# Router of a mixture-of-experts layer: x2 turned in contiguous runs, the last tile's first half turned early, its row scaling behind the expert choice

## Chip, cores and metric

One core of one Trainium2 chip runs the whole kernel. The time is device microseconds of one launch. The engines are TensorE (PE in the rows, PEld for its weight loads), VectorE (DVE), ScalarE (ACT), GpSimd (POOL) and SyncE (SP); the last two also issue the DMAs, each on a queue of its own.

## What is computed

A two-part encoder layer on 512 prompt rows and 256 sample rows of 1024 channels, 768 rows in all: six tiles of 128 rows. The first part (projection, differential attention, retention, merge, output projection) ends in the residual sum x2. The second part is a mixture of 32 experts, and the change sits at the seam between the two:

```
x = x + token_mixer(rmsnorm(x, attn_norm_g), ...)          # this sum is x2
xt = rmsnorm(x, ffn_norm_g)
lg = xt @ w_rg + b_rg                                      # 4 groups: the best one
le = einsum('td,gde->tge', xt, w_re) + b_re                # 8 experts in it: the best two
h = silu(xb @ w1[e]) * (xb @ w3[e]);  y = (h @ w2[e]) * gate
out = x + sum of a token's two experts;  then a last rmsnorm
```

## The kernel before

The program is written engine by engine, and each engine runs its list in the order written. Semaphores join the lists: s_w counts finished halves of the output projection, s_x2 halves of x2, s_rTm and s_rTc halves of x2 turned and copied, s_lg logits, s_rx logits scaled on VectorE, s_rr scaled rows, s_nb the finished routing tables.

**The output projection and the router's logits** run tile by tile, t from 0 to 5. TensorE sums each half n of a tile (512 columns, 24 matmuls: each operand is split into a high and a low part, L584 to L586) in PSUM bank 6 or 7. VectorE adds the residual row by row (L1561), which is x2. TensorE turns x2 with eight 128x128 transposes (`route_columns`, L772 to L780), four into bank 0 and four into bank 1; the slice of each has a stride of 8 elements, `x2[t % 3][:, 4 * j + c::KC]`. ScalarE copies each bank into `rT` (`route_copy`, L1108 to L1114). Eight small matmuls give the 36 logits of each row in bank 2 (`logits`, L782 to L791), and VectorE scales them by the row's 1/rms and adds the bias (`route_logits`, L1502). `logits` waits on s_rx, since bank 2 has to be read before it is written again. In the loop, `route_columns(t-1)` stands behind the first half of tile t and `logits(t-1)` in the middle of its second half; the last tile's turns and logits come behind the loop. The router's weights are laid out on the host, and multiplied on GpSimd by the norm's gains (`gcol`, L1724).

**The scaled rows.** ScalarE squares a tile's x2 (L1127), VectorE works out 1/rms (`rsqrt_column`, nine small operations from L1242) and writes the scaled rows `rrow` (L1568), and GpSimd stores them twice in DRAM (`xn_scratch`, L1728). In the list of VectorE the row scaling of tile t stands ahead of the logits of tile t-1; for the last tile both logits follow it:

```
dve.scalar_tensor_tensor(out=rrow[t % 2][:, :], in0=x2[t % 3][:, :], ...).then_inc(s_rr, 1)
if t >= 1:
    route_logits(t - 1)
...
route_logits(NT - 1)
choose(NT - 2, NT)
```

**The choice.** `choose` (L1509 to L1548) picks each row's experts: for tiles 0 to 3 ahead of the last tile's sum, for tiles 4 and 5 at the end. TensorE counts rows per expert (`count`, L829 and L833), VectorE works out slots and one-hot tables (L1582 to L1604), TensorE turns them into the index table (L844), and VectorE writes it (`idxt`, L1622). Three idle matmuls (`keep_busy`, L825) run ahead of the wait for it.

**The first block of the expert stage.** GpSimd gathers 64 pairs of half rows by `idxt` (L1748), TensorE turns them (L859), VectorE copies them (`xT`, L1639), and TensorE starts on w1 and w3 (L869). The weights come through `rawe`, a ring of three experts, 2 MB per matrix, issued by SP (L520). SP issues expert 1 (6 MB) once the last half of the projection is summed (s_w), behind it the store of the last tile's x2 (`x2_out`, L536, 0.5 MB), then, after s_rr, w1 of expert 2, and the rest after the first gather. ScalarE copies the first expert's weights out of the ring: half of w1 and w3 (`first_up(0)`, L1131), then w2 (L1143), then two exponentials for the gates, then the other half. The first of these copies waits for all stores of x2, because it writes over x2's buffer; the second waits for the stores of the scaled rows. VectorE computes the gates (L1625 to L1629) ahead of the `xT` copy of the first block. The stage then runs 41 blocks, of which each needs w1, w3 and w2 of its expert.

Of the kernel before, what the change touches and what calls it, by code (L numbers as in the profile page):

```python
# [19 lines left out]
ALU = mybir.AluOpType  # L20
# [3 lines left out]
P = 128  # L24
D = 1024
KC = D // P
SEQS = (512, 256)
T = sum(SEQS)
NT = T // P
# [6 lines left out]
NG, EPG = 4, 8  # L36
NE = NG * EPG
# [63 lines left out]
def hybrid_layer(nc, A):  # L101
# [19 lines left out]
    x2 = [at(f"x2{s}", D_O + (32 + 4 * s) * KB, [P, D]) for s in range(3)]  # L121
# [15 lines left out]
    rstd = small("rstd", [P, 48])  # L137
# [59 lines left out]
    g2 = at("g2", D_O + 16 * KB, [P, D])  # L197
    rT = at("rT", D_O + 44 * KB, [P, KC, P])
    rrow = [at(f"rrow{s}", F_O + (16 + 4 * s) * KB, [P, D]) for s in range(2)]
    wrt = at("wrt", F_O + 36 * KB, [P, KC, NG + NE])  # L200
    brt = at("brt", F_O + 36 * KB + 1280, [P, NG + NE])
    gcol = at("gcol", F_O + 36 * KB + 1152, [P, KC])
# [36 lines left out]
    ps = [ctx.enter_context(nc.psum_tensor(f"ps{i}", [P, 512], F32)) for i in range(8)]  # L239
# [4 lines left out]
    ident = C("ident")  # L244
# [11 lines left out]
    with ctx:  # L256
# [58 lines left out]
        s_x2 = sem("s_x2")  # L315
        s_x2s = [sem(f"s_x2s{s}") for s in range(3)]
        s_x2l = sem("s_x2l")
        s_rp = sem("s_rp")
# [3 lines left out]
        s_rr = sem("s_rr")  # L322
        s_rst = [sem(f"s_rst{s}") for s in range(2)]
        s_rTm = sem("s_rTm")
# [92 lines left out]
        def _(sp):  # L417
# [89 lines left out]
            for k in range(2, 2 * NT):  # L507
                gate_half(k)
                if k in (3, 4, 11):
                    p = {3: 5, 4: 6, 11: 7}[k]  # L510
# [3 lines left out]
            sp.dma_start(g2[:, :], A["ffn_norm_g"].partition_broadcast(P)[:, 0, :]).then_inc(s_rp, 16)  # L514
            sp.dma_start(wrt[:, :, :], A["router_w"].rearrange("(p c) n -> p c n", c=KC)).then_inc(s_rp, 16)
            sp.dma_start(brt[:, :], A["router_b"].rearrange("(a n) -> a n", a=1).partition_broadcast(P)[:, 0, :]).then_inc(s_rp, 16)
            sp.dma_start(gcol[:, :], A["ffn_norm_g"][0].rearrange("(p c) -> p c", c=KC)).then_inc(s_rp, 16)
            def weight(x, slot, k, done):
                c = slot * EW + k * 2 * PIECE
                sp.dma_start(rawe[:, c:c + 2 * PIECE].rearrange("p (h n) -> p h n", h=2),  # L520
# [60 lines left out]
        def _(pe):  # L581
# [187 lines left out]
                        mm = pe.transpose(ps[4 + n % 2][:, c * P:(c + 1) * P], mg[t][:, 4 * j + c::KC], ident)  # L769
                    mm.then_inc(s_mT, 1)  # L770

            def route_columns(t):  # L772

                pe.wait_ge(s_x2, 2 * t + 2)
                if t >= 1:
                    pe.wait_ge(s_rTc, 2 * t)
                for j in range(2):
                    for c in range(4):
                        mm = pe.transpose(ps[j][:, c * P:(c + 1) * P], x2[t % 3][:, 4 * j + c::KC], ident)
                    mm.then_inc(s_rTm, 1)  # L780

            def logits(t):  # L782
                pe.wait_ge(s_rTc, 2 * t + 2)
                if t == 0:
                    pe.wait_ge(s_wrg, 1)
                if t >= 1:
                    pe.wait_ge(s_rx, t)
                for c in range(KC):
                    mm = pe.matmul(ps[2][:, 0:NG + NE], rT[:, c, :], wrt[:, c, :],
                                   start=(c == 0), stop=(c == KC - 1))  # L790
                mm.then_inc(s_lg, 1)  # L791
            merged_to_columns(0)
            for t in range(NT):
                if t + 1 < NT:
                    merged_to_columns(t + 1)
                pe.wait_ge(s_mTl, 2 * t + 2)
                for n in range(2):
                    if t >= 1:
                        pe.wait_ge(s_x2, 2 * t + n - 1)
                    for j in range(2):  # L800
                        p = 2 * n + j
                        if t == 0:
                            pe.wait_ge(s_lo, ZP + 4 + p + 1)
                        for k in range(4):
                            c = 4 * j + k
                            mm = split_mm(ps[6 + n][:, :], mTh[t % 2][:, c, :], mTl[t % 2][:, c, :],
                                          m_hi[4 + p][:, k * 512:(k + 1) * 512],
                                          m_lo[4 + p][:, k * 512:(k + 1) * 512],
                                          c == 0, c == KC - 1)
                        if t == NT - 1 and j == 0:  # L810
                            mm.then_inc(s_pe, 1)
                        if t >= 1 and n == 1 and j == 0:
                            logits(t - 1)
                    mm.then_inc(s_w, 1)
                    if t >= 1 and n == 0:
                        route_columns(t - 1)
            route_columns(NT - 1)


            picked = Ab[:, :, :].rearrange("p t e -> p (t e)")  # L820
# [92 lines left out]
        def _(act):  # L913
# [191 lines left out]
                    act.activation(mTh[t % 2][:, 4 * j:4 * j + 4, :].rearrange("p c k -> p (c k)"),  # L1105
                                   ps[4 + n % 2][:, :], ACT.Copy).then_inc(s_mTh, 1)

            def route_copy(t):  # L1108
                for j in range(2):
                    act.wait_ge(s_rTm, 2 * t + j + 1)  # L1110
                    if t >= 1:
                        act.wait_ge(s_lg, t)
                    act.activation(rT[:, 4 * j:4 * j + 4, :].rearrange("p c k -> p (c k)"),
                                   ps[j][:, :], ACT.Copy).then_inc(s_rTc, 1)  # L1114
# [3 lines left out]
            for t in range(NT):  # L1118
                if t + 1 < NT:
                    merged_hi(t + 1)  # L1120
                if t >= 1:
                    route_copy(t - 1)

                act.wait_ge(s_x2, 2 * t + 2)
                if t >= 2:
                    act.wait_ge(s_rst[t % 2], 16 * (t // 2))
                act.activation(rrow[t % 2][:, :], x2[t % 3][:, :], ACT.Square, accum_out=ssq[:, t:t + 1]).then_inc(s_sq2, 1)  # L1127
            route_copy(NT - 1)

            def first_up(h):  # L1130
                act.activation(cur13[h][:, :, :], rawe[:, 0:4 * PIECE].rearrange("p (k n) -> p k n", k=2)  # L1131
# [80 lines left out]
        def _(dve):  # L1212
# [289 lines left out]
            def route_logits(t):  # L1502
                dve.wait_ge(s_lg, t + 1)
                dve.scalar_tensor_tensor(out=lg[:, t, :], in0=ps[2][:, 0:NG + NE], scalar=rstd[:, t:t + 1],
                                         in1=brt[:, :], op0=ALU.mult, op1=ALU.add).then_inc(s_rx, 1)
# [3 lines left out]
            def choose(a, b):  # L1509
# [36 lines left out]
                                              op0=ALU.mult, op1=ALU.add))  # L1546
                pick(A12[:, 1, a:b, :], v[:, 6, :])
                dve.tensor_tensor(Ab[:, a:b, :], A12[:, 0, a:b, :], A12[:, 1, a:b, :], ALU.add).then_inc(s_Ab, 1)  # L1548
            BIG = 1.0e30
            for t in range(NT):  # L1550
                if t + 1 < NT:
                    merged_lo(t + 1)
                else:
                    choose(0, NT - 2)
                dve.wait_ge(s_xr[t % 3], 16 * (t // 3 + 1))
                for n in range(2):
                    dve.wait_ge(s_w, 2 * t + n + 1)
                    if t >= 3 and n == 0:
                        dve.wait_ge(s_rTm, 2 * (t - 2))
                        dve.wait_ge(s_x2s[t % 3], 16)  # L1560
                    dve.tensor_tensor(x2[t % 3][:, n * 512:(n + 1) * 512], ps[6 + n][:, :],  # L1561
                                      xres[t % 3][:, n * 512:(n + 1) * 512], ALU.add).then_inc(s_x2, 1)

                dve.wait_ge(s_sq2, t + 1)
                rsqrt_column(t, D)
                if t == 0:
                    dve.wait_ge(s_rp, 16 * 4)
                dve.scalar_tensor_tensor(out=rrow[t % 2][:, :], in0=x2[t % 3][:, :], scalar=rstd[:, t:t + 1],  # L1568
                                         in1=g2[:, :], op0=ALU.mult, op1=ALU.mult).then_inc(s_rr, 1)
                if t >= 1:  # L1570
                    route_logits(t - 1)

            route_logits(NT - 1)
            choose(NT - 2, NT)
            dve.memset(zero[:, :], 0.0).then_inc(s_ini, 1)
            dve.wait_ge(s_ini, 1)
            link(dve.tensor_tensor(v6[:, 2, :], v6[:, 6, :], v6[:, 5, :], ALU.subtract))
# [234 lines left out]
```

## Time and profile before

| | us |
|---|---|
| median of 3 runs | 1207.0 (1206.47 to 1207.01) |
| the profiled execution, its own time | 1205.33 |
| its span, first to last instruction | 1203.5 |
| TensorE busy | 1093.9 (91%) |
| VectorE busy | 520.1 (43%) |
| ScalarE busy | 400.6 (33%) |
| GpSimd busy | 189.1 (16%) |

The profiled execution is one run; what it took beyond its span is 1.8 us. Busy shares are means over all stages. A row of the timeline has the start in us, the time in us, the engine, the line, the operation, output <- input, the shape and the count; in brackets stands the idle time just before it and what ended it. A row of the chain has the start, the time and what the end of the program was waiting for in that stretch.

### The profile page before, as it was taken

How to read it: one execution, taken by the hardware profiler on the slowest of the kernel's cores; microseconds unless marked ns; L12 is line 12 of the kernel's file. 1: busy time of each engine (PE TensorE's matmuls, PEld its weight loads, DVE VectorE, ACT ScalarE, POOL GpSimd, SP SyncE). 2: the span in 40 equal slices, each digit the busy share in tenths (PEclk: the TensorE clock that was granted, in tenths of full speed). 3: DMA queues.
4: the chain of work that ended last, by engine and by line, in shares of the span. 5: the costliest groups of instructions: out<-in, count | busy, mean ns of one | idle time of the engine just before them, and what ended most of it. 6: DMA issues, size and time to landing. Idle time of an engine off the chain costs nothing.

```text
span 1203.5 us, 15505 instructions
## 1 busy us (share of the span) xinstructions
PE 1093.9 (91%) x5142; PEld 660.6 (55%) x5142; DVE 520.1 (43%) x893; ACT 400.6 (33%) x629; POOL 189.1 (16%) x236
## 2 busy tenths in 40 slices
PE   5899999999999998999977999999998798999960
PEld 4688888888876667878863333333333233333320
DVE  5651522111027898563354435352443343341518
ACT  5322233222135666112214243424143323333232
POOL 0110011011000000000001232333233323232210
PEclk9999999999999999999987999999999999999995
DMA  8733331621341005448358899999999999999546
GB/s 312 256 123 123 114 122 48 240 104 44 139 170 58 1 2 175 158 152 360 123 219 357 351 422 419 419 420 420 420 413 420 421 421 419 419 422 419 225 158 260
DMA packets 69248, 308.89 MB, mean 257 GB/s; under 512 B 9024, under 2 KB 9152, under 8 KB 43872
## 3 DMA queue, kind: packets, MB, share of 16 engines
q1 hardware_dynamic: 56144, 273.86, 57.2%
q0 software_dynamic: 13072, 34.63, 7.4%
q8 instruction: 17, 0.28, 0.1%
q14 instruction: 15, 0.12, 0.0%
HBM read 278.57 MB, written 39.06 MB: 264 GB/s over the span
## 4 chain that ended last, share of the span: by engine, by line
PE 69%; DMA 14%; DVE 9%; ACT 4%; issue 3%; SPq 1%; DVEq 0%; ACTq 0%; POOLq 0%; POOL 0%
PE ps L869 18%; PE ps L584 12%; PE ps L586 12%; PE ps L585 12%; DMA rawe<-in_w 10%; PE ps L896 8%; DMA x_scratch<-x 2%; PE ps L859 2%; DVE cur13b L1662 1%; PE ps L878 1%; ACT prob L1013 1%; DMA xrow<-in_x_sample 1%; DVE att L1366 1%; ACT cur L1194 1%; DMA ya<-y_scratch 1%
## 5 line engine op out<-in xcount | busy, mean ns | idle before, releaser
L584 PE MATMUL ps<-whi,xTh 128*128 128x512 f32 x480 | 188.4, 393 | 18.1 <-DVE wlo L1225 13.8
L585 PE MATMUL ps<-wlo,xTh 128*128 128x512 f32 x480 | 187.9, 392 | 0.0
L586 PE MATMUL ps<-whi,xTl 128*128 128x512 f32 x480 | 187.9, 391 | 0.0
L869 PE MATMUL ps<-cur13a,xT 128*64 128x512 f32 x656 | 157.5, 624 | 2.0 <-DVE xT L1639 1.7
L1662 DVE COPY cur13a<-rawe 128x4096 f32 x31 | 71.2, 2296 | 191.3 <-DMA rawe<-in_w 99.7
L869 PE MATMUL ps<-cur13b,xT 128*64 128x512 f32 x656 | 147.8, 592 | 0.0
L896 PE MATMUL ps<-cur,hT 128*64 128x512 f32 x640 | 146.2, 598 | 0.0
L1194 ACT ACTIVATE cur<-rawe 128x4096 f32 x31 | 112.1, 3618 | 3.7 <-issue 1.4
L584 PEld LDWEIGHTS ps<-whi,xTh 128*128 128x128 f32 x480 | 91.0, 190 | 37.3 <-issue 18.5
L963 ACT ACTIVATE zst<-ps,rstd 128x512 f32<-128x512 f32 x60 | 41.1, 687 | 208.0 <-PE ps L586 205.9
L585 PEld LDWEIGHTS ps<-wlo,xTh 128*128 128x128 f32 x480 | 91.0, 189 | 19.1
L586 PEld LDWEIGHTS ps<-whi,xTl 128*128 128x128 f32 x480 | 90.8, 189 | 19.0
L869 PEld LDWEIGHTS ps<-cur13b,xT 128*64 128x64 f32 x656 | 47.8, 137 | 93.0 <-issue 93.0
L869 PEld LDWEIGHTS ps<-cur13a,xT 128*64 128x64 f32 x656 | 46.1, 143 | 83.0 <-issue 77.0
L1225 DVE TENSOR_TENSOR wlo<-raw,whi 128x2048 fp32r<-128x2048 f32 x20 | 45.8, 2292 | 104.2 <-ACT whi L919 103.3
L1744 POOL COPY idxb<-idxt 128x1 int32 (+1 forms) x40 | 45.4, 1135 | 241.9 <-PE ps L859 241.9
L896 PEld LDWEIGHTS ps<-cur,hT 128*64 128x64 f32 x640 | 42.4, 136 | 73.4 <-issue 68.5
L1721 POOL DMA_DIRECT2D z_scratch<-zst x60 | 32.9, 548 | 316.5 <-ACT zst L963 171.6
L1662 DVE COPY cur13b<-rawe 128x4096 f32 x31 | 71.1, 2292 | 23.3 <-PE ps L869 23.2
L1176 ACT ACTIVATE ystage<-ps 128x512 f32<-128x512 f32 x41 | 24.5, 597 | 159.3 <-PE ps L896 159.3
L1639 DVE COPY xT<-ps 128x512 f32<-128x512 f32 x41 | 28.1, 684 | 84.8 <-PE ps L859 84.8
L1164 ACT ACTIVATE sg<-ps 128x256 f32<-128x256 f32 x41 | 15.7, 383 | 141.4 <-PE ps L869 141.4
(212 smaller groups left out, 1382.6 us busy)
## 6 DMA issues: line engine op xcount, KB each, us to landing
rawe<-in_w SPq DMA_DIRECT2D x96, 2048.0 KB, 25.9
raw<-in_w_in SPq DMA_DIRECT2D x20, 1024.0 KB, 6.2
z_scratch<-zst POOLq DMA_DIRECT2D x60, 256.0 KB, 2.3
gat<-z_scratch SPq DMA_DIRECT2D x12, 512.0 KB, 3.8
xn_scratch<-rrow POOLq DMA_DIRECT2D x6, 1024.0 KB, 5.2
ya<-y_scratch SPq DMA_DIRECT2D x6, 1024.0 KB, 10.7
raw<-in_w_out SPq DMA_DIRECT2D x4, 1024.0 KB, 6.6
xcol<-in_x_cols SPq DMA_DIRECT2D x6, 512.0 KB, 10.2
```

What stands on the lines that cost most here:

```text
L584: pe.matmul(out, ah, bh, start=first, stop=False)
L585: pe.matmul(out, ah, bl, start=False, stop=False)
L586: return pe.matmul(out, al, bh, start=False, stop=last)
L869: mm = pe.matmul(ps[0][u * CAP:(u + 1) * CAP, :], xT[:, c, h * CAP:(h + 1) * CAP], cur13[h][:, :, c * 512 + u * 256:c * 512 + u * 256 + 25 ...
L896: mm = pe.matmul(ps[6][u * CAP:(u + 1) * CAP, :], hT[:, k, h * CAP:(h + 1) * CAP], w2, start=(h == 0 and k == 0), stop=(h == 1 and k == 1))
L963: act.activation(zst[k][:, :], ps[k][:, :], ACT.Sigmoid if c >= 6 else ACT.Copy, scale=rstd[:, t:t + 1]).then_inc(s_zev, 1)
L1194: act.activation(cur2[:, :], rawe[:, bass.ds((e % RING) * EW + 4 * PIECE, 2 * PIECE)], ACT.Copy).then_inc(s_cw2, 1)
L1225: dve.tensor_tensor(elo[slot][:, :], raw[slot_raw][:, :], hi[:, :].bitcast(F32), ALU.subtract).then_inc(s_lo, 1)
L1639: dve.tensor_copy(xT[:, :, :].rearrange("p c k -> p (c k)"), ps[2][:, :]).then_inc(s_xt, 1)
L1662: dve.tensor_copy(cur13[h][:, :, :], pair[:, :, h * PIECE:(h + 1) * PIECE]).then_inc(s_c13, 1)
L1721: pool.dma_start(z_d[t * P:(t + 1) * P, c * 512:(c + 1) * 512], zst[k][:, :]).then_inc(s_zst[k], 16)
L1744: pool.tensor_copy(idxb[:, :], idxt[:, bass.ds(b, 1)]).then_inc(s_ic, 1)
```

## The change

The transposes of x2 read runs of 128 columns in place of every eighth column; the router's weights and gains are laid out on the host to match. `route_columns` takes a half. For the last tile its first half is turned in the middle of the last half's sum, behind `logits(4)`, and ScalarE copies it before it squares that tile's rows. On VectorE `route_logits(4)` moves up between the two residual sums of the last tile, and the row scaling of the last tile moves behind the second `choose`.

```diff
-            sp.dma_start(gcol[:, :], A["ffn_norm_g"][0].rearrange("(p c) -> p c", c=KC)).then_inc(s_rp, 16)
+            sp.dma_start(gcol[:, :], A["ffn_cols"].rearrange("(p c) -> p c", c=KC)).then_inc(s_rp, 16)
...
-            def route_columns(t):
-
-                pe.wait_ge(s_x2, 2 * t + 2)
+            def route_columns(t, j):
+
+                pe.wait_ge(s_x2, 2 * t + j + 1)
                 if t >= 1:
                     pe.wait_ge(s_rTc, 2 * t)
-                for j in range(2):
-                    for c in range(4):
-                        mm = pe.transpose(ps[j][:, c * P:(c + 1) * P], x2[t % 3][:, 4 * j + c::KC], ident)
-                    mm.then_inc(s_rTm, 1)
+                for c in range(4):
+                    mm = pe.transpose(ps[j][:, c * P:(c + 1) * P], x2[t % 3][:, (4 * j + c) * P:(4 * j + c + 1) * P], ident)
+                mm.then_inc(s_rTm, 1)
...
                         if t >= 1 and n == 1 and j == 0:
                             logits(t - 1)
+                            if t == NT - 1:
+                                route_columns(t, 0)
                     mm.then_inc(s_w, 1)
                     if t >= 1 and n == 0:
-                        route_columns(t - 1)
-            route_columns(NT - 1)
+                        route_columns(t - 1, 0)
+                        route_columns(t - 1, 1)
+            route_columns(NT - 1, 1)
...
-            def route_copy(t):
-                for j in range(2):
+            def route_copy(t, halves=(0, 1)):
+                for j in halves:
...
                 if t >= 1:
                     route_copy(t - 1)
+                if t == NT - 1:
+                    route_copy(t, (0,))
...
-            route_copy(NT - 1)
+            route_copy(NT - 1, (1,))
...
+            def rows_scaled(t):
+                dve.scalar_tensor_tensor(out=rrow[t % 2][:, :], in0=x2[t % 3][:, :], scalar=rstd[:, t:t + 1],
+                                         in1=g2[:, :], op0=ALU.mult, op1=ALU.mult).then_inc(s_rr, 1)
...
                                       xres[t % 3][:, n * 512:(n + 1) * 512], ALU.add).then_inc(s_x2, 1)
+                    if t == NT - 1 and n == 0:
+                        route_logits(t - 1)
...
-                dve.scalar_tensor_tensor(out=rrow[t % 2][:, :], in0=x2[t % 3][:, :], scalar=rstd[:, t:t + 1],
-                                         in1=g2[:, :], op0=ALU.mult, op1=ALU.mult).then_inc(s_rr, 1)
-                if t >= 1:
-                    route_logits(t - 1)
+                if t < NT - 1:
+                    rows_scaled(t)
+                    if t >= 1:
+                        route_logits(t - 1)
 
             route_logits(NT - 1)
             choose(NT - 2, NT)
+            rows_scaled(NT - 1)
...
-        [inputs["w_rg"][0][:, None, order], inputs["w_re"][0][order].transpose(1, 2, 0)], axis=1).reshape(D, NG + NE))
+        [inputs["w_rg"][0][:, None, order], inputs["w_re"][0][order].transpose(1, 2, 0)], axis=1).reshape(KC, P, NG + NE).transpose(1, 0, 2).reshape(D, NG + NE))
+    laid["ffn_cols"] = _np.ascontiguousarray(inputs["ffn_norm_g"][0].reshape(KC, P).T.reshape(D))
```

TensorE before, in the middle of the last half of tile 5 (`wrt,rT` are the logits of tile 4, `mhi`, `mlo` the projection's weights, `x_75` is x2 of tile 5):

```order
L789 MATMUL ps<-wrt,rT 128x36 [waits s_rx,s_rTc]
L789 MATMUL ps<-wrt,rT 128x36 x7
L584 MATMUL ps<-mhi_155,mTh_70 128x512
L585 MATMUL ps<-mlo_160,mTh_70 128x512
L586 MATMUL ps<-mhi_155,mTl_72 128x512
```

The same place in the changed kernel:

```order
L788 MATMUL ps<-wrt,rT 128x36 [waits s_rx,s_rTc]
L788 MATMUL ps<-wrt,rT 128x36 x7
L778 MATMUL ps<-cst,x_75 128x128 [waits s_rTc,s_x2]
L778 MATMUL ps<-cst,x_75 128x128 x3
L584 MATMUL ps<-mhi_155,mTh_70 128x512
L585 MATMUL ps<-mlo_160,mTh_70 128x512
L586 MATMUL ps<-mhi_155,mTl_72 128x512
```

Four of the eight transposes of tile 5 now stand, with a wait for the first half of x2, ahead of the last 12 matmuls of the projection.

VectorE before, from the first choice's end over the last tile's two residual sums (the nine small operations of 1/rms follow them):

```order
L1548 TENSOR_TENSOR Ab<-A_175 128x128 [waits s_dv]
L1561 TENSOR_TENSOR x_75<-ps,xres_165 128x512 [waits s_rTm,s_x2s2,s_w,s_xr2]
L1561 TENSOR_TENSOR x_75<-ps,xres_165 128x512 [waits s_w]
L1242 TENSOR_SCALAR rs_a<-ssq 128x1 [waits s_sq2]
L1243 TENSOR_SCALAR ssq<-ssq 128x1
```

and behind 1/rms:

```order
L1247 SCALAR_TENSOR_TENSOR rstd<-rs_a,rstd 128x1 [waits s_dv]
L1568 SCALAR_TENSOR_TENSOR rrow_169<-x_75,rstd,g_166 128x1024 [waits s_dv]
L1504 SCALAR_TENSOR_TENSOR lg<-ps,rstd,brt 128x36 [waits s_lg] x2
L1522 TENSOR_REDUCE v_93<-lg 128x2 [waits s_rx]
L1523 TENSOR_TENSOR gq<-lg,v_93 128x8 [waits s_dv]
```

VectorE in the changed kernel, from the same first row:

```order
L1552 TENSOR_TENSOR Ab<-A_175 128x128 [waits s_dv]
L1568 TENSOR_TENSOR x_75<-ps,xres_165 128x512 [waits s_rTm,s_x2s2,s_w,s_xr2]
L1508 SCALAR_TENSOR_TENSOR lg<-ps,rstd,brt 128x36 [waits s_lg]
L1568 TENSOR_TENSOR x_75<-ps,xres_165 128x512 [waits s_w]
L1246 TENSOR_SCALAR rs_a<-ssq 128x1 [waits s_sq2]
```

and from the second choice's end:

```order
L1552 TENSOR_TENSOR Ab<-A_175 128x64 [waits s_dv]
L1554 SCALAR_TENSOR_TENSOR rrow_169<-x_75,rstd,g_166 128x1024
L1585 MEMSET zero 128x32
L1587 TENSOR_TENSOR v_93<-v_93 128x6 [waits s_ini]
L1592 TENSOR_SCALAR wint<-ps 128x32 [waits s_dv,s_rk]
```

The logits of tile 4 are scaled before the second sum, and the row scaling (L1554 in the changed kernel) stands between the choice and the slot arithmetic.

## Rows read from the trace of the kernel before

**Rows 1.** The chain that ended last, from the projection's end to the second weight copy.

```profile
617.77 0.38 SPq L520
...
619.22 20.09 DMA x_scratch<-x
...
639.42 0.06 ACT cur13a L1131
...
642.94 0.14 ACT cur L1143
```

**Rows 2.** The timeline of TensorE, 612 to 650 us.

```profile
613.02 1.87 PE L789 MATMUL ps<-wrt,rT 128*128 128x36 f32 x16
...
618.52 1.16 PE L779 MATMUL ps<-cst,x 128*128 128x128 f32 x8 [0.78 <-DVE x L1561]
...
623.06 1.95 PE L789 MATMUL ps<-wrt,rT 128*128 128x36 f32 x16 [1.90 <-DVE lg L1504]
...
647.15 0.75 PE L859 MATMUL ps<-cst,xg 128*128 128x128 f32 x4 [0.36 <-DMA xg<-xn_scratch,idxt]
649.65 3.65 PE L869 MATMUL ps<-cur13a,xT 128*64 128x512 f32 x16 [1.75 <-DVE xT L1639]
```

**Rows 3.** The timeline of VectorE, 614 to 643 us.

```profile
614.65 0.68 DVE L1561 TENSOR_TENSOR x<-ps,xres 128x512 f32<-128x512 f32 x1
...
621.46 1.28 DVE L1568 SCALAR_TENSOR_TENSOR rrow<-x,rstd,g 128x1024 f32<-128x1024 f32 x1
...
625.05 0.26 DVE L1504 SCALAR_TENSOR_TENSOR lg<-ps,rstd,brt 128x36 f32<-128x36 f32 x1 [2.13 <-PE ps L789]
...
631.42 0.19 DVE L1582 TENSOR_SCALAR wint<-ps 128x32 uint32<-128x32 f32 x1 [1.34 <-PE ps L833]
...
642.45 0.28 DVE L1622 TENSOR_SCALAR idxt<-ps,cst 128x56 int32<-128x56 f32 x1 [1.26 <-PE ps L844]
```

**Rows 4.** The timelines of ScalarE and GpSimd, 618 to 645 us.

```profile
619.55 1.06 ACT L1113 ACTIVATE rT<-ps 128x512 f32<-128x512 f32 x2
...
623.04 0.68 POOL L1728 DMA_DIRECT2D xn_scratch<-rrow  x1 [12.95 <-DVE rrow L1568]
...
643.68 1.10 POOL L1748 DMA_INDIRECT xg<-xn_scratch,idxt  x1 [7.13 <-DVE idxt L1622]
```

**Rows 5.** Landing of L1728's stores, then queues (packets, MB, share) in 626 to 635 us.

```profile
DMA to landing us min/median/max: 4.4/5.2/12.9
...
q1 hardware_dynamic: 335, 2.61, 73.2%
q0 software_dynamic: 265, 1.04, 28.1%
```

**Rows 6.** Stretches: busy PE, PEld, DVE, ACT, POOL, then PEclk, DMA share, GB/s.

```profile
625.00:646.00 21.00, 11.65 (x38) 8.52 (x38) 13.91 (x66) 6.58 (x2) 1.62 (x2) 0.51 0.91 368
660.00:662.00 2.00, 2.00 (x6) 0.47 (x4) 0.00 (x0) 0.00 (x1) 0.00 (x0) 0.50 1.01 426
690.00:1132.00 442.00, 420.57 (x1908) 149.31 (x1906) 173.75 (x161) 149.73 (x168) 130.49 (x141) 0.98 1.00 414
```

**Rows 7.** The chain in the first blocks of the expert stage.

```profile
659.49 8.70 PE ps L869 x32
...
672.89 7.02 PE ps L869 x32
```

**Rows 8.** SP's own waits, 600 to 700 us.

```profile
SPq L520 <- ACT cur L1194: 17.3, 1, 17.3
```

**Rows 9.** Turns of x2 (L779) and of z (L627): the chain's steps, then weight loads in ns.

```profile
609.55 0.88 PE ps L779 x8
...
348.30 7.87 PE ps L627 x72
...
L779 PEld LDWEIGHTS ps<-cst,x x48: 185/188/208, 551.8 to 619.3; 128*128 128x128 f32 x48
...
L627 PEld LDWEIGHTS ps<-cst,zqk x48: 138/141/143, 347.9 to 354.9; 128*128 128x128 f32 x48
```

## The prediction

> **What bounds the kernel now.** I began at the end and asked what has to be earlier for the program to end earlier. In the windows from 690 to 1132 us the DMA share is 1.00, at 414 GB/s [rows 6]: the expert stage is a weight stream with full queues. Such a stream ends earlier only if it starts earlier. SP's own waits tell what starts it: after the first experts SP stood 17.3 us until ScalarE had copied w2 out of the ring [rows 8], a copy that stands behind the first blocks' matmuls. So a shift of the first block (the `xT` copy, then L869 at 649.65) reaches the end one for one, and nothing ahead of it counts unless it moves that start.
>
> Two branches lead to the first block, and the change speaks to one of them.
>
> Branch A, the routing: residual sum, turns, logits, choice, counts, tables. TensorE's logits of tile 5 start at 623.06 after an idle 1.90 us that VectorE's scaling of the logits of tile 4 ended [rows 2]; VectorE scales those of tile 5 at 625.05, has waited 1.34 us for the counts at 631.42, and writes `idxt` from 642.45 to 642.73 [rows 3]. GpSimd issues the gather at 643.68 [rows 4], TensorE turns the rows from 647.15 to 647.90 and then waits 1.75 us [rows 2].
>
> Branch B, the weights of the first expert: the chain of work that ended last goes this way [rows 1]. The last matmul of the projection lets SP issue expert 1 at 617.77, three transfers of 2 MB; the store of the last x2 is issued behind them at 619.22 and takes 20.09 us. ScalarE then copies from 639.42 and from 642.94, computes the exponentials, VectorE the gates, and only then comes `xT`. From landing (639.31) to the first L869 (649.65) are 10.3 us, all in series. Branch A had its columns ready at 647.90, and the first L869 follows such a point by an `xT` copy of 0.7 us: A has about 1.0 us of slack. B ends last.
>
> **The change, part by part.**
>
> The order of the columns. The projection's stage is bound by TensorE, so 40 transposes of tiles 0 to 4 lie on its path. Eight strided ones step in 0.88 us, 110 ns each; 72 contiguous ones of the earlier stage in 7.87 us, 109 ns each [rows 9]. Worth 0. The strided loads do take longer (188 against 141 ns) but run beside the matmul ahead.
> [...]
>
> The transposes inside the last sum. Tile 4's logits end at 613.02 + 1.87 = 614.89 [rows 2] and the last 12 matmuls followed at once. The first half of x2 is done only at 614.65 + 0.68 = 615.33, since VectorE runs the first choice ahead of it [rows 3]. TensorE now waits 0.44 us, then 0.06 to start and 4 x 0.11 to turn, with some 0.1 for the start of a group (eight after a wait took 1.16 for 0.88): the last sum ends **1.1 us later** (0.9 to 1.3), 618.9. This is on branch B: s_w lets SP issue expert 1, and everything of B is behind it.
>
> The routing. x2's second half is 1.1 later (619.6). ScalarE squares (1.2 us) and copies one half, not two (1.06 us for two [rows 4]): `rT` is complete at about 621.3. The logits of tile 4 are scaled already at 615.6, between the two sums, where VectorE idles. So TensorE's logits of tile 5 start at 621.4 and not 623.06, and the scaling that was at 625.05 comes at 623.4: 1.6 us earlier. The moved row scaling (1.28 us [rows 3]) lies in the 1.34 us for which VectorE waits for the counts; without this cover it would cost 1.3. `idxt` is done at about 641.1, **1.6 us earlier**. This is branch A, which had slack: worth nothing by itself.
>
> The scaled rows. They end at 629.6 instead of 622.74, so GpSimd's store of 1 MB is issued at 629.8, not 623.04 [rows 4], and SP's w1 of expert 2, behind s_rr, as much later; the queue is full of expert 1 until about 637, so that load loses no time. The store took 12.9 us where its kind takes 5.2 [rows 5]. As long it would land at 642.7, when w1 alone is left beside it; I take 641. ScalarE's second copy, which waits for it, can't start before 643.7; the gather, which waits for it too, needs it by about 641. Hidden, or nearly.
>
> The last x2's store. In 626 to 635 us the scaled rows' queue moved 1.04 MB and SP's 2.61 MB [rows 5]: the 1 MB store goes through ahead of x2's. In the changed kernel it starts about 6.7 us later, at 633, and has moved about 7 us x 1.04/9 = 0.8 MB when x2's store lands. What is not yet moved, 0.2 MB at some 0.4 MB/us, gives back 0.5 us, and less if the two stores alternate more evenly. Landing is later by 1.1 - 0.5 to 1.1: I take **+0.8 us**, 640.1.
>
> The sum. Branch B: 640.1 + 10.3 = 650.4 for the first L869. Branch A: gather at 642.1, columns 4.2 us later (as from 643.68 to 647.90) at 646.3, or 647.3 beside the stream. B still ends last, and the program is later by 0.8 us. The profiled execution's 1205.33 becomes 1206.1; it lay 1.7 below the median of the runs, and the median 1207.0 becomes **1207.8 us**. About 0.2% (2.4 us) is what a measurement of this kernel can tell from no change, so this is no change that shows.
>
> **The rivals.**
>
> A colder first block (slower). TensorE's granted clock stood at 0.51 of full through 625 to 646, and again at 0.50 in 660 to 662 [rows 6]: the latter after a block with TensorE idle for part of it, and it made the 32 matmuls of block 2 8.70 us instead of 7.02 [rows 7], 1.7 us. With A earlier and B later, TensorE idles 4 us ahead of the first L869 where it idled 1.75. [...] For it: this longer idle time. Against it: the clock held at full from 646 on with 1.75 us of idling.
>
> Late rows (slower, and plainly so). The store of the scaled rows now starts late; if it lands more than 14 us after its issue (643.8), first ScalarE's w2 copy, soon the gather wait for it, and each us beyond costs one. At 17 us it is 3 us on top of nothing else: 1210.8. For it: 12.9 us last time. Against it: by then expert 1 is through, and less stands beside it.
>
> The store of x2 gets ahead (faster). If the scaled rows' packets start later than I assume, x2's store passes before nearly all of them: 1.05 MB less at 0.4 MB/us is 2.5 us less, +1.1 - 2.5 = -1.4, and A allows it, being 1.6 earlier: 1205.5. The same time comes out if, against the chain, the routing ended last. It speaks for it that x2's transfer stands in the queue before the rows are even issued; against it that at 633 some 3 us of expert 1 are still ahead.
>
> Strides cost (faster). If the steps hide a price that the loads show, 47 ns for each of 44 transposes on TensorE's path are 2.1 us, and the time is 1205.7. Rows 9 speak against it.
>
> **How the numbers follow.** Forecast 0.60, a colder first block 0.14, late rows 0.06, x2's store ahead 0.15, strides 0.05. The forecast's own bounds are +0.3 to +1.4, with the scatter of the runs (0.5) 1206.8 to 1208.8. The range reaches to the colder block above and to the two faster cases below: 1205.0 to 1209.8. Slower by over 0.2% (above 1209.4) are half of the colder blocks and most late rows, 0.13; faster (below 1204.6) is a faster case with a clock that doesn't fall in block 2, 0.05; the rest, 0.82, is within.
>
> **What would show it.** Right: the four turns inside the last sum behind 0.4 us of waiting, SP's expert 1 at 618.9, logits of tile 5 on VectorE at 623.4, `idxt` at 641.1, x2's store landing at about 640, L869 at 650.4 with TensorE idle for 4 us ahead of it, and the chain through the store of x2. Wrong: a chain through `xn_scratch` or the gather; L869 before 649; a window at clock 0.50 after 650; a number of blocks other than 41, since the new order of the sums could turn a near tie in the router.

## The result, and the profile after

| | before | changed |
|---|---|---|
| median of 20 runs, us | 1206.85 (1203.79 to 1208.97) | 1210.19 (1206.92 to 1212.60) |
| ratio, with its 95% interval | | 1.0028 [1.0019, 1.0037] |
| the profiled execution, us | 1205.33 | 1208.01 |
| its span, us | 1203.5 | 1206.2 |

The kernel became slower by 0.28%, outside the range, and the likeliest case of the prediction (+0.8 us, nothing to be seen) did not happen. The profiled execution shows how. All times below stand against one anchor that every version has: the start of TensorE's logits of tile 4, 613.02 us in the kernel before [rows 2] and 613.31 in the changed one. Ahead of it the programs do the same work. "The first block" is, on TensorE, its 32 matmuls of w1 and w3.

TensorE's timeline of the changed kernel, from that anchor to the first block:

```profile
613.31 1.87 PE L788 MATMUL ps<-wrt,rT 128*128 128x36 f32 x16
...
615.69 0.66 PE L778 MATMUL ps<-cst,x 128*128 128x128 f32 x4 [0.51 <-DVE x L1568]
...
619.89 0.66 PE L778 MATMUL ps<-cst,x 128*128 128x128 f32 x4 [0.79 <-DVE x L1568]
...
621.87 1.95 PE L788 MATMUL ps<-wrt,rT 128*128 128x36 f32 x16
...
647.07 0.75 PE L861 MATMUL ps<-cst,xg 128*128 128x128 f32 x4 [0.77 <-DMA xg<-xn_scratch,idxt]
651.54 5.97 PE L871 MATMUL ps<-cur13a,xT 128*64 128x512 f32 x16 [3.73 <-DVE xT L1649]
```

Second and third row: four turns stand inside the last sum behind a wait of 0.51 us, four behind it. Fourth row: the logits of tile 5 start 8.6 us behind the anchor, 10.0 before. Then the two differences that matter: the first block waits 3.73 us for `xT` where it waited 1.75 [rows 2], and its first 16 matmuls take 5.97 us where they took 3.65.

The chain that ended last, of the changed kernel:

```profile
620.59 20.62 DMA x_scratch<-x
...
651.54 9.41 PE ps L871 x32
...
663.71 7.02 PE ps L871 x32
```

It goes through the store of the last x2 as before [rows 1], and the transit (issue to landing) is 20.62 us, not 20.09. The 32 matmuls of the first block take 9.41 us. In the chain of the kernel before they took 7.09:

```profile
649.65 7.09 PE ps L869 x32
```

Those of the second block take 7.02 us and not 8.70 [rows 7]. The windows show why (columns as in [rows 6]):

```profile
646.00:649.40 3.40, 1.04 (x5) 0.56 (x4) 0.62 (x4) 3.40 (x4) 0.79 (x1) 1.00 0.53 135
649.40:652.80 3.40, 1.26 (x4) 0.53 (x6) 0.95 (x3) 3.23 (x2) 0.24 (x1) 0.51 0.97 407
652.80:656.20 3.40, 3.40 (x10) 0.95 (x8) 0.00 (x0) 1.02 (x2) 0.00 (x0) 0.50 1.02 421
656.20:659.40 3.20, 3.20 (x16) 0.98 (x14) 0.00 (x0) 0.00 (x0) 0.00 (x0) 0.99 1.02 433
```

The second of these windows in the kernel before:

```profile
649.40:652.80 3.40, 3.15 (x16) 1.16 (x18) 0.19 (x1) 2.36 (x3) 0.31 (x1) 1.00 0.95 398
```

The granted clock is back at full at 646 in both kernels (1.00 over 646.00 to 649.40). In the changed one TensorE then idles, and at 649.4 the clock falls to 0.50 of full and stays there until 656.

The routing did what it should, and the scaled rows are late as planned:

```profile
641.24 0.28 DVE L1632 TENSOR_SCALAR idxt<-ps,cst 128x56 int32<-128x56 f32 x1 [1.25 <-PE ps L846]
```

```profile
630.23 0.68 POOL L1738 DMA_DIRECT2D xn_scratch<-rrow  x1 [19.85 <-DVE rrow L1554]
641.98 0.52 POOL L1744 MEMSET xg<- 128x512 f32 x1 [11.07 <-DMA xn_scratch<-rrow]
643.49 1.10 POOL L1758 DMA_INDIRECT xg<-xn_scratch,idxt  x1 [0.98 <-POOL xg L1744]
```

The first row is of VectorE's timeline, the others are of GpSimd's. VectorE scales the rows at 628.66, and GpSimd issues their store at 630.23. `idxt` starts 27.93 us behind the anchor, 29.43 before [rows 3]: 1.5 us earlier. The gather starts only 0.5 us earlier against the anchor (30.2 for 30.7 [rows 4]): GpSimd cleared its tile only once the scaled rows had landed.

### The profile page after: what moved, and what is told of

Same layout as the page of the kernel before. It is cut to its first block, busy times and chain, and to the rows that moved or that the text cites. A ratio compares the mean times of both kernels' runs of the same rounds, so it can differ in the third digit from the quotient of the medians.

```text
span 1206.2 us, 15511 instructions
## 1 busy us (share of the span) xinstructions
PE 1097.5 (91%) x5142; PEld 661.8 (55%) x5142; DVE 520.1 (43%) x893; ACT 400.7 (33%) x629; POOL 192.4 (16%) x236
## 4 chain that ended last, share of the span: by engine, by line
PE 67%; DMA 15%; DVE 10%; issue 4%; ACT 3%; SPq 1%; DVEq 0%; ACTq 0%; POOLq 0%; POOL 0%
PE ps L871 18%; PE ps L584 12%; PE ps L586 12%; PE ps L585 12%; DMA rawe<-in_w 11%; PE ps L898 7%; DMA x_scratch<-x 2%; PE ps L861 1%; DVE cur13b L1672 1%; PE ps L880 1%; ACT prob L1015 1%; DMA xrow<-in_x_sample 1%; DVE att L1370 1%; DMA ya<-y_scratch 1%; DVE mx L1357 1%
## 5 line engine op out<-in xcount | busy, mean ns | idle before, releaser
L871 PE MATMUL ps<-cur13a,xT 128*64 128x512 f32 x656 | 160.8, 635 | 4.0 <-DVE xT L1649 3.7
L1168 ACT ACTIVATE sg<-ps 128x256 f32<-128x256 f32 x41 | 15.7, 384 | 144.8 <-PE ps L871 144.8
## 6 DMA issues: line engine op xcount, KB each, us to landing
ya<-y_scratch SPq DMA_DIRECT2D x6, 1024.0 KB, 10.6
```

Source lines behind the costliest of these rows:

```text
L871: mm = pe.matmul(ps[0][u * CAP:(u + 1) * CAP, :], xT[:, c, h * CAP:(h + 1) * CAP], cur13[h][:, :, c * 512 + u * 256:c * 512 + u * 256 + 25 ...
```

## The experiments

The same five readings stand for every run: start of the first block's matmuls behind the anchor, idle time of TensorE just ahead of them, time of the first and the second block's 32 matmuls (from the chain, or, where the chain leaves the block out, from the timeline), and the rest of the span behind the anchor (the profiled span less the anchor). A block is called cold where its matmuls ran in part at the lower clock (0.50 of full in the windows), warm where they took 7.0 to 7.1 us. The part ahead of the anchor took 612.8 to 617.2 us in the profiled executions, though it is the same work in all: in some the granted clock was still at 0.50 in 45 to 48 and in 366 to 369 us (`logits_only`), in others at 1.00 (`after_warm`). It adds scatter to every median and says nothing of the change; so a profile is compared by the last column, and the medians decide. The last column is one execution each, and scatters too: `best_busy` and `best_busy_again` are one program, with 586.3 and 588.5.

| run | first block at | idle ahead | block 1, block 2 | rest of span | ratio to before, interval |
|---|---|---|---|---|---|
| before | 36.63 | 1.75 | 7.09, 8.70 | 590.5 | |
| changed | 38.23 | 3.73 | 9.41, 7.02 | 592.9 | 1.0028 [1.0019, 1.0037] |
| columns_only | 36.65 | 1.72 | 8.62, 7.02 | 590.5 | 1.0000 [0.9991, 1.0010] |
| turn_only | 37.66 | 0.94 | full speed, 7.02 | 589.9 | 1.0015 [1.0002, 1.0027] |
| logits_only | 36.67 | 3.85 | 10.00, 8.71 | 592.9 | 1.0029 [1.0017, 1.0042] |
| rows_only | 36.36 | 2.10 | 10.06, 8.71 | 593.1 | 1.0016 [1.0004, 1.0029] |
| after_warm | 38.11 | 1.12 | 7.09, 7.02 | 590.3 | 1.0009 [0.9995, 1.0023] |
| logits_warm | 36.66 | 1.35 | 7.09, 7.02 | 589.4 | 1.0002 [0.9993, 1.0011] |
| store_first_before | 35.53 | 0.78 | full speed, 7.02 | 589.6 | 1.0009 [1.0000, 1.0018] |
| logits_store_first | 34.32 | 0.78 | full speed, 7.02 | 588.7 | 0.9991 [0.9980, 1.0002] |
| no_early_turn | 37.01 | 3.79 | 9.63, 7.02 | 592.3 | 1.0036 [1.0023, 1.0048] |
| rows_ahead | 37.80 | 3.98 | 9.12, 7.02 | 592.2 | 1.0043 [1.0030, 1.0056] |
| best_busy | 34.03 | 0.78 | full speed, 7.02 | 586.3 | 0.9989 [0.9977, 1.0001] |
| best_stream | 37.69 | 0.78 | 9.19, 7.02 | 592.1 | 1.0034 [1.0021, 1.0047] |
| no_early_warm | 37.20 | 1.42 | 7.09, 7.02 | 589.4 | 0.9988 [0.9978, 0.9998] |
| no_busy | 36.61 | 1.48 | 8.70, 7.02 | 590.5 | 1.0013 [0.9997, 1.0029] |
| best_busy_again | 34.33 | 0.78 | full speed, 7.02 | 588.5 | 0.9986 [0.9974, 0.9998] |

**The four parts, one at a time.** Theory at this point: the turns inside the last sum delay SP's transfers. Rivals: the late store of the scaled rows, and the clock.

`columns_only`, the new column order alone, with both halves of the last tile turned behind the sum (the diff is against the changed kernel):

```diff
-                            if t == NT - 1:
-                                route_columns(t, 0)
...
+            route_columns(NT - 1, 0)
             route_columns(NT - 1, 1)
```

The matching edit on ScalarE and the two edits on VectorE are undone as well.

> Only the order of the columns changes, with the laid out weights; both halves of the last tile are turned behind the sum and both other edits are undone. If the steps of the transposes are what counts (110 ns for eight, as for contiguous ones): the same time as before, the first L869 at 649.5 to 650, and weight loads of the turns at 141 instead of 188 ns that buy nothing. If strides cost TensorE time: 2 us faster. If the new layout itself is what made the changed kernel slower: 3 us slower.

1207.24 us, ratio 1.0000. The column order costs and gives nothing. In its profile the clock fell to 0.50 at about 649.9 and was back at 1.00 from 653.6, and the first block took 8.62 us, behind 1.72 us of idling; in the kernel before the clock held through 1.75.

`turn_only`, the same with the first half turned inside the last sum:

> Contiguous columns and the first half of the last tile turned inside the last sum; the logits of tile 4 and the row scaling stay where they were before. First theory (the wait and the four turns inside the sum delay SP's expert 1 and the store of x2 behind it): the last sum ends 1.1 us later than in the kernel before, the store lands 1.1 later, the first L869 starts 1.1 later, the time is 1 to 1.5 us longer. Rival (the late store of the scaled rows does the harm): within 0.3 us of before in the landing after correcting for the sum, and the loss of the changed kernel mostly absent.

1208.80 us, +0.15% [0.02, 0.27]. The first block starts 37.66 us behind the anchor, 1.03 later than in the kernel before, with a transit of 20.1: the first theory's 1.1 us is there. The routing is late too, since tile 5's logits start 1.1 us later and take 2.87 us for 1.95; the two branches end within 0.2 us of each other, and the chain names the routing. The scaled rows were stored ahead of the choice here, so a late store of them is not the cause. That the 1.1 us alone make the 0.15% is not shown: in the profile block 2 ran warm and the rest of the span is 0.6 us shorter than before, and the runs fall in two groups, 5 at 1205.6 to 1207.2 with a mean granted clock of 0.964 to 0.966, and 7 at 1208.1 to 1211.6 with 0.959 to 0.964, as would come of a clock that falls in some runs.

`logits_only`, the kernel before with tile 4's logits scaled between the sums:

```diff
                                       xres[t % 3][:, n * 512:(n + 1) * 512], ALU.add).then_inc(s_x2, 1)
+                    if t == NT - 1 and n == 0:
+                        route_logits(t - 1)
...
-                if t >= 1:
+                if 1 <= t < NT - 1:
                     route_logits(t - 1)
```

> The kernel before with one edit: the logits of tile 4 are scaled between the two residual sums of the last tile. First theory: the routing tables end 2.2 us earlier (about 640.5) and nothing follows, since the store of x2 lands at 639.3 as before and the first L869 stays at 649.7: time the same. Rival (the clock): TensorE idles 2 us longer ahead of the first block, its clock falls there more often, and the median is 0.5 to 1.7 us longer with the same start of the first block.

1211.12 us: +0.29% [0.17, 0.42], the whole loss of the changed kernel from an edit that only removes waiting. Its chain and a window of it:

```profile
622.98 20.14 DMA x_scratch<-x
...
653.45 10.00 PE ps L869 x32
```

```profile
653.00:659.00 6.00, 5.55 (x14) 1.71 (x16) 0.40 (x1) 2.57 (x3) 0.00 (x0) 0.50 1.02 425
```

The transit of the store and the start of the first block (36.67) are those of before. All that moved on the way to it is the routing, and with it TensorE's idle time, 3.85 us for 1.75; the first block takes 10.00 us, with the clock at 0.50 in 653 to 659. The rival with the clock is what happened, at more than its upper price.

`rows_only`, the kernel before with the last row scaling behind the choice (its old place is dropped):

```diff
             choose(NT - 2, NT)
+            rows_scaled(NT - 1)
```

> The kernel before with one edit: the row scaling of the last tile stands behind the second choice. The tables end 1.3 us earlier, the store of the scaled rows is issued about 6.5 us later. First theory by the bytes ahead of it: the store of x2 lands 0 to 0.5 us earlier and the time is the same or 0.5 us less. Rival (the two stores clash, as a transit of 20.6 in place of 20.1 us in the changed kernel suggests): x2's store lands 0.5 us later or more and the time is 0.5 to 1 us longer.

1208.72 us, +0.16% [0.04, 0.29]. The transit was 19.83 us and the first block 0.3 earlier, so the two stores did not clash. But the time is 1.5 us longer, which neither theory had: the first block is cold again (10.06). TensorE idled only 2.10 us just ahead of it. The clock fell to 0.50 with this and with 1.72 us in `columns_only`, and held at 1.00 with 1.75 in the kernel before, so the length of the last idle stretch does not decide by itself whether it falls.

**The clock held up.** `after_warm` and `logits_warm` put three idle matmuls into the gap:

```diff
             rows_to_columns(0)
+            keep_busy(3)
             up(0)
```

> The changed kernel with three idle matmuls (the same as the three behind the index tables, on bank 7) between the turns of the first gathered rows and the first block: they fill the 3.7 us for which TensorE idles there. Theory of the clock: the first block runs at full clock, 7.1 instead of 9.4 us, though it starts no earlier (38.2 us behind the logits of tile 4), and the median falls by 1.5 to 2.5 us to about 1208, 0.5 to 1.5 above the kernel before, which is what the turns in the last sum and the longer transit cost. Rival (the transfers: the late store of the scaled rows holds up the store of x2, and this is the whole loss): no gain, 1210.

> The kernel before with the logits of tile 4 scaled early, and the same three idle matmuls ahead of the first block. Theory of the clock: the 0.3% that the early scaling alone had lost is gone, the first L869 starts 36.7 us behind the logits of tile 4 and takes 7.1 us for 32; time within 0.1% of before, or a little under where the second block keeps the clock too. Rival (the early tables hurt in another way, as by a gather that collides with the weight stream): still 3 to 4 us above before.

```profile
646.46 0.75 PE L861 MATMUL ps<-cst,xg 128*128 128x128 f32 x4 [0.72 <-DMA xg<-xn_scratch,idxt]
647.04 2.74 PE L827 MATMUL ps<-cst 128*128 128x512 f32 x6
650.90 3.65 PE L871 MATMUL ps<-cur13a,xT 128*64 128x512 f32 x16 [1.12 <-DVE xT L1650]
```

These are TensorE's rows of `after_warm`: the fillers take 2.74 us, the block starts as late as in the changed kernel (38.11) and runs at 3.65 us per 16 matmuls. The median was 1206.81, against 1206.70 of the kernel before measured beside it: +0.09% [-0.05, 0.23], 1.1 us, within the forecast's 0.5 to 1.5. For `logits_warm` it was +0.02% [-0.07, 0.11], and 0.29% without the fillers. Nothing but idle matmuls was added, the first block started within about 0.1 us of where it did without them, and both blocks ran at full clock (granted 1.00, 7.09 and 7.02 us), so the loss was the clock. The kernel before with the same fillers was not run; as its own second block was cold (8.70), part of what the fillers gave here they might give there too.

**What is left without it.** `no_early_turn` is the changed kernel without the turns in the last sum, `rows_ahead` the changed kernel with the row scaling back ahead of the logits of tile 5.

> The changed kernel with both halves of the last tile turned behind the sum, as before; early logits of tile 4 and late row scaling stay. If the turns inside the sum cost 1.1 us on the branch of the store and the cold first block costs the rest: the first L869 starts 36.4 to 37.2 us behind the logits of tile 4 (38.2 in the changed kernel), the first block is still cold (about 10 us), and the time is 1 us under the changed kernel's, near 1209. Rival (the turns are harmless, the clock is all): 1210 as the changed kernel.

> The changed kernel with the last tile's row scaling back ahead of the logits of tile 5. The scaled rows are stored 5 us earlier, ahead of the last x2. If the late store of the rows lengthened the transit of x2's store by 0.5 us: transit 20.1, first L869 at 37.7 behind the logits of tile 4, the clock still low in the first block, and 0.5 us under the changed kernel, 1209.5. Rival (the transit is chance): 20.5 as in the changed kernel and the same 1210.

Both starts came as expected or near it (37.01, and 37.80 with a transit of 20.2), both first blocks were cold, and both medians (1210.52 of 6 runs and 1211.34 of 5) are above the changed kernel's, where 1209 and 1209.5 were expected: two misses. A cold first block cost 1.5 to 3.0 us over all profiles, depending on when the clock falls and rises (1.5 where it was at 0.50 from 649.9 to 653.3, `columns_only`; 3.0 where it was from 651.8 to 658.6, `rows_only`), and that can hide a difference of 0.5 or 1 us. Inconclusive by themselves; hence the pair with a warm block:

> The changed kernel without the turns inside the last sum and with three idle matmuls ahead of the first block. If both causes are real (clock, and the turns' 1.1 us): the first L869 starts 37.0 us behind the logits of tile 4 against 38.1 with the turns, takes 7.1 us, and the median is 0.5 to 1 us under that of the same kernel with the turns, at the level of before (ratio 1.000). Rival (only the clock matters): the same as with the turns, 1.0009.

1206.06 us, ratio 0.9988 [0.9978, 0.9998]. The same kernel with the turns (`after_warm`) has 1.0009 [0.9995, 1.0023]: the turns cost 0.2% between them, somewhat more than their 0.9 us of start; the intervals overlap a little, so this is likely and not clear of noise. Without the turns and with the fillers the changed kernel is faster than the one before, which had no such fillers.

`no_busy` takes the kernel before and drops its own three idle matmuls:

```diff
-            keep_busy(3)
             pe.wait_ge(s_nb, 1)
```

> The kernel before without its three idle matmuls behind the index tables. No transfer and no start changes: L869 at 36.6 us behind the logits of tile 4. Theory of the clock: it is still low when the first block starts, the first block takes about 10 us instead of 7.1, and the median is 2 to 3 us longer, as large a loss as the changed kernel's. Rival (the clock matters little, since the weight stream bounds): within 0.5 us of before.

The start stayed at 36.61, the clock was at 0.50 at it, and the first block took 8.70 us, less than forecast. The median is 1207.32, +0.13% [-0.03, 0.29], with runs from 1203.53 to 1213.04: unclear. In its profile the clock rose some 3 us into the block (0.50 up to 655.2, 1.00 from 655.6) and then held in the second: the two blocks together take 15.7 us, 15.8 before. So my "10 us" was wrong as a rule: a block's price depends on where in it the clock rises (8.70 us here with the rise 3.3 us after its start, 10.00 in `logits_only` with the rise at 5.9). And this run does not bear out the theory's 2 to 3 us.

**The store first.** The chain names the store of x2 behind 6 MB of weights. Put ahead of them:

```diff
             sp.wait_ge(s_w, 2 * NT)
-            expert(1, EPG * ORDER[1])
             sp.wait_ge(s_x2, 2 * NT)
             x2_out(NT - 1)
+            expert(1, EPG * ORDER[1])
```

> The kernel before with one edit on SP: the store of the last x2 is issued ahead of expert 1 instead of behind it. Theory (the store's 20.1 us behind 6 MB end last): it lands within 5 us, ScalarE's copies are done long before they are wanted, and the routing ends last: the first L869 starts 1.0 us earlier, TensorE idles 0.8 us and not 1.75 ahead of it, and the time is 1 to 2 us shorter. Rival (the routing ended last all the time): the same start of L869 and the same time, or 0.7 longer, as expert 1 is issued 0.7 us later.

The trace did as the theory said: the first block starts 1.1 us earlier with 0.78 us of idling, and the chain turns to the routing tables and the gather. The median did not follow: +0.09% [0.00, 0.18], a miss. The chain of `store_first_before` shows the next wait:

```profile
644.83 3.41 DMA xg<-xn_scratch,idxt
...
649.81 7.56 DMA xg<-xn_scratch,idxt
```

The second gather now runs beside the full weight stream (mean DMA share 0.93 over it, 0.41 over the first), 7.56 us for the first's 3.41, and it, not the first block, sets the second block's start. Why the median was not lower at all stays open.

> Both the early scaling of tile 4's logits and the store of x2 ahead of expert 1, no turns in the last sum and no moved row scaling. Theory: with the store out of the way the routing bounds the first block, and the 2.2 us that the early scaling gives are worth their time: the first L869 starts about 33.5 us behind the logits of tile 4 (36.6 before), with TensorE idle for about 1 us ahead of it, and the time is 3 us below before, some 1204. Rival: the gather meets the weight stream and gives back 1 us, and the clock, which rose at 645.8 in the kernel before, hasn't risen when the first block starts: 1207.

1206.29 us, -0.09% [-0.20, 0.02]: the first block starts 34.32 us behind the anchor (33.5 expected), 2.3 earlier than before. The time missed the theory's 1204 and lies near the rival's 1207: of the 2.3 us, 0.4 show in the medians measured side by side. In the profile the third block starts 3.3 us earlier, since block 2 ran warm, and the rest of the span is 1.8 shorter; where the difference goes was not followed. Against `store_first_before` (1.0009), measured beside it, the early logits are worth 0.18%.

**Versions that try for more.** `best_busy` adds to it one idle matmul inside the first block, where TensorE waits for the hidden rows:

```diff
             rows_to_columns(1)
+            pe.matmul(ps[7][:, 0:3 * P], ident, cst[:, 0:3 * P], start=True, stop=True)
             hidden_to_columns(0)
```

> Early logits of tile 4, the store of x2 ahead of expert 1, and one idle matmul of 384 columns while TensorE waits for the first block's hidden rows, which keeps the clock up for the second block. With the start of the first block at 34.3 us behind the logits of tile 4: 1205 to 1206, 1 us under before. Rival: the stream's restart behind the first gather is what bounds now, so the matmul buys nothing: 1206.3 as without it.

> The same program as best_busy, for its interval: 1.2 us under before again if the first time was not chance, ratio near 0.999; 1.000 if it was.

1204.89 and 1205.36 us, ratios 0.9989 [0.9977, 1.0001] and 0.9986 [0.9974, 0.9998]: the same program twice, some 0.12% under the kernel before and, by the ratios, 0.4% under the changed one. The second interval stands clear of 1, the first includes it. The times are as expected; that the idle matmul made them is not shown, as block 2 was warm without it too (`logits_store_first`, 7.02 and ratio 0.9991).

`best_stream` also lets SP go on with expert 2 without waiting for the first gather:

> The same, and SP issues w3 and w2 of expert 2 without waiting for the first gather, so that the weight stream has no gap of some 2 to 4 us there. If the stream's restart bounds the end: 2 us less, 1204. Rival: the gather is slowed by the stream from 4 to 7.5 us, the first block starts 3 us later, TensorE idles and cools ahead of it, and the time is the same or up to 3 us longer.

The chain of this version:

```profile
645.02 7.19 DMA xg<-xn_scratch,idxt
...
654.17 9.19 PE ps L868 x32
```

1210.37 us, +0.34% [0.21, 0.47]: the rival's mechanism, at more than its 3 us (4.2 above the kernel before, 5.5 above `best_busy`). The gather takes 7.19 us in the chain instead of 4.07 (`best_busy`), with a mean DMA share of 1.02 over it instead of 0.79, TensorE idles 3.6 us ahead of the turns of the gathered rows, the first block starts 3.7 us later and is cold (9.19).

## Why the prediction was wrong

**What bounds the kernel.** Right. The chain went through the store of x2 again, and `idxt` gained 1.5 us (forecast 1.6) that bought nothing. The scaling of tile 5's logits came 10.6 us behind the anchor against 12.0. The reading of SP's waits was incomplete: it took the 17.3 us for the copy of w2 [rows 8], and the same view has a longer one,

```profile
SPq L520 <- DMA xg<-xn_scratch,idxt: 24.0, 1, 24.0
```

so the weight stream starts again behind the first gather, which is on the routing branch. In `logits_warm` this gather was issued 2.2 us earlier, with both blocks warm, and the time was +0.02%: no gain is seen from it.

**The column order.** Right: ratio 1.0000. In `columns_only` the weight loads of the turns became shorter (140 ns for 188) and their matmuls did not (273 ns each in both), so the time is the same.

**The transposes inside the last sum.** Right: a wait of 0.51 us (0.50 forecast with its 0.06), SP's expert 1 issued at 619.14, which is 1.1 us later against the anchor. `turn_only` has +0.15%, of which the clock's share is not known.

**"The last x2's store", +0.8 us.** Mis-sized: the first block came 1.6 us later against the anchor. Of that 1.1 are the turns; the transit grew by 0.5 us where the term gave back 0.3. With the row scaling alone moved it did shrink (19.8). It was 20.5 to 20.7 in all four versions with both early tables and late rows, 20.2 with the rows early. Why the transit is longer in that combination was not isolated.

**"A colder first block", given 0.14.** This is the step that failed. The mechanism and its place were named, TensorE's idle time (forecast 4 us, found 3.73) too, but it was treated as a side risk of the 1.7 us that block 2 had lost before (1209.5 with it), while the forecast's sum assumed a warm block and put the clock at nothing; measured it was 2.3 us (9.41 for 7.09). In the profiles the first block was cold in all four versions with 3.7 to 4.0 us of idling ahead of it and no fillers (9.1 to 10.0 us for 32 matmuls, 2.0 to 2.9 above 7.09), and warm in all three with fillers there. The argument "the clock held at full from 646 on with 1.75 us of idling" spoke of one execution of the kernel before and not of twice that idling; in `columns_only` and `rows_only` the first block was cold with 1.72 and 2.10. With the clock's price added to the 1.6 us of the start, less the 1.7 us that the second block no longer loses, 1.6 + 2.3 - 1.7 = 2.2 of the 2.4 us are explained by which the rest of the span grew (592.9 for 590.5).

**Medians.** The medians differ by 3.3 us, the profiles by 2.4 behind the anchor. The profiled execution of before had paid 1.7 us in its second block; `columns_only`, whose program is the same in time, had paid 1.5 in its first. How often each happens over the runs is not in the traces, so the last us is argued, not shown.

**The other rivals.** Late rows did not happen: they landed 11.6 us after their issue (14 was the bound). They delayed the gather by about 1 us inside A's slack, as GpSimd's clearing of the gather's tile waited for them, a step that the prediction left out. The store of x2 did not get ahead, and the strides cost nothing (`columns_only`, 1.0000). The forecast's upper bound is 0.1 too low by its own terms (1207.0 + 1.4 + 0.5 = 1208.9).

## What to carry to other kernels

An edit that shortens a branch with slack can cost time: here it lengthened TensorE's idle time ahead of its next dense stage, and the lower clock cost 2.3 us where the turns and the longer transit cost 1.6 together (and 0.29% of the time came from one moved 0.25 us instruction). When a stage's start is fixed by something else, look at how long TensorE idles ahead of it and at the granted clock there, and fill the gap with idle matmuls, or remove the wait that fixes the start; then the early work did no harm (1.0002 for the early logits with fillers) or paid: 0.9988 with fillers and without the turns in the sum, 0.9989 and 0.9986 with the store first. How much of these gains the fillers alone would bring the kernel before was not tested. Work put inside a sum that a transfer queue waits for delayed the whole queue by its wait and its length (1.1 us here).

## What the runs showed of the hardware

TensorE's granted clock fell from 1.00 to 0.50 1.6 us after the last turn in the changed kernel and cost its next 32 matmuls 2.3 us (9.41 for 7.09); three idle matmuls of 2.74 us in the gap kept it at 1.00 in all three programs that had them. With idle stretches of 1.7 to 2.1 us ahead of the block it held in one profile (before, 1.75) and fell in two (`columns_only`, 1.72, and `rows_only`, 2.10). In the chains a gather of the first two blocks took 3.41 us with a mean DMA share of 0.41 over it (`store_first_before`), 4.06 to 4.24 with 0.79 to 0.81 (`best_busy`, `best_busy_again`, `logits_store_first`), and 7.19 to 8.11 with 0.93 to 1.02, beside the weight stream; in `best_stream` the slower gather made keeping the stream going a loss (1.0034). With the 1 MB store of the scaled rows late, the transit of x2's store was 19.83 (`rows_only`) to 20.67 us (`no_early_warm`) in the profiles, against 20.09 before; what it depends on was not isolated.
